# Gate projection of a mixer layer as two units of seven block products

## The reference

```python
u = rms_norm(h, g_mix)
z = u @ w_in                     # columns: q_a k_a v_a | q_b k_b v_b | f_b | gate_logits (2 x 1024)
y_a = sliding_window_attention(q_a, k_a, v_a, sinks) @ w_br_swa
y_b = forgetting_attention(q_b, k_b, v_b, f_b + b_forget) @ w_br_fox
gates = sigmoid(gate_logits)     # (tokens, 2, 1024)
mixed = gates[:, 0] * y_a + gates[:, 1] * y_b
h = h + mixed @ w_mix_out
```

## Time and profile before

| | us |
|---|---|
| median of 3 runs | 1800.6 (1798.06 to 1803.86) |
| profiled execution, its own time | 1800.78 |
| its span, first to last instruction | 1799.0 |
| TensorE busy | 1758.1 (98% of the span) |
| VectorE busy | 1027.4 (57%) |
| ScalarE busy | 671.0 (37%) |
| GpSimd busy | 266.1 (15%) |

### The profile page before, as it was taken

The page is one execution under the profiler, slowest core; times in us unless marked ns, Lnnn a source line. Parts: engine busy times, 40 slices in busy tenths (PEclk is TensorE's granted clock), DMA queues, the critical chain, the costliest instruction groups (busy, mean ns, idle before and its releaser), DMA issues.

```text
span 1799.0 us, 21080 instructions
## 1 busy us (share of the span) xinstructions
PE 1758.1 (98%) x8533; PEld 1479.4 (82%) x8533; DVE 1027.4 (57%) x1377; ACT 671.0 (37%) x1049; POOL 266.1 (15%) x350
## 2 busy tenths in 40 slices
PE   7999999999899999999999999999999999999998
PEld 7888888888899888887888888888887788888886
DVE  5432144432798444489957965984887256445423
ACT  4322244442798431453223323323344234222212
POOL 2000021210687125100000000000002132000101
PEclk9999999999999999999999999999999999999999
DMA  5434524214662454175173246227211112111232
GB/s 177 135 109 138 176 82 129 83 59 113 157 142 48 140 183 180 46 277 180 65 260 120 94 166 255 75 76 290 98 47 36 49 69 100 65 52 43 72 115 94
DMA packets 107600, 215.65 MB, mean 120 GB/s; under 512 B 7984, under 2 KB 28016, under 8 KB 105072
## 3 DMA queue, kind: packets, MB, share of 16 engines
q1 hardware_dynamic: 107504, 214.31, 35.7%
HBM read 170.21 MB, written 44.07 MB: 119 GB/s over the span
## 4 chain that ended last, share of the span: by engine, by line
PE 85%; DVE 5%; DMA 3%; ACT 2%; POOL 2%; issue 1%; SPq 1%; POOLq 0%; ACTq 0%; DVEq 0%
PE PS L649 16%; PE PS L651 16%; PE PS L650 16%; PE PS L883 10%; PE PS L884 10%; PE PS L885 10%; PE PS L625 3%; DVE WB L1705 1%; PE PS L753 1%; POOL TF L1990 1%; PE PS L798 1%; DMA kb_scratch<-STG 1%; SPq L2084 1%; DVE PFL L1379 1%; DMA KO<-kb_scratch 1%
## 5 line engine op out<-in xcount | busy, mean ns | idle before, releaser
L649 PE MATMUL PS<-UH,RHL 128*128 128x512 f32 (+1 forms) x768 | 294.3, 383 | 4.1 <-DVE UL L1379 2.2
L651 PE MATMUL PS<-UH,RHL 128*128 128x512 f32 (+1 forms) x768 | 290.3, 378 | 0.0
L650 PE MATMUL PS<-UL,RHL 128*128 128x512 f32 (+1 forms) x768 | 290.2, 378 | 0.0
L989 ACT ACTIVATE WH<-WB 128x2048 fp32r<-128x2048 f32 x56 | 107.3, 1916 | 295.1 <-PE PS L885 239.7
L1379 DVE TENSOR_TENSOR WB<-WB,WH 128x2048 fp32r<-128x2048 f32 x56 | 128.2, 2290 | 99.6 <-ACT WH L989 99.6
L883 PE MATMUL PS<-WH,AH 128*128 128x512 f32 x448 | 175.0, 391 | 4.0 <-DVE H L1666 2.3
L883 PE MATMUL PS<-AH,WH 128*128 128x512 f32 x448 | 174.6, 390 | 0.0
L885 PE MATMUL PS<-WH,AL 128*128 128x512 f32 x448 | 174.4, 389 | 0.0
L884 PE MATMUL PS<-WB,AH 128*128 128x512 f32 x448 | 174.3, 389 | 0.0
L885 PE MATMUL PS<-AH,WB 128*128 128x512 f32 x448 | 174.3, 389 | 0.0
L884 PE MATMUL PS<-AL,WH 128*128 128x512 f32 x448 | 174.3, 389 | 0.0
(11 more groups left out here) (219 smaller groups left out, 3249.5 us busy)
## 6 DMA issues: line engine op xcount, KB each, us to landing
WB<-in_w_ff SPq DMA_DIRECT2D x32, 1024.0 KB, 9.2
AH<-uf_scratch SPq DMA_DIRECT2D x21, 1024.0 KB, 5.3
AL<-uf_scratch SPq DMA_DIRECT2D x21, 1024.0 KB, 7.5
RAW<-in_w_in SPq DMA_DIRECT2D x32, 512.0 KB, 3.6
H<-in_x SPq DMA_DIRECT2D x16, 512.0 KB, 9.2
gates_scratch<-GST SPq DMA_DIRECT2D x32, 256.0 KB, 2.2
G<-gates_scratch SPq DMA_DIRECT2D x32, 256.0 KB, 2.9
RAW<-in_pool_in_w SPq DMA_DIRECT2D x16, 512.0 KB, 3.2
```

What stands on the lines that cost most here:

```text
L649: pe.matmul(o_ap, sh, mh, start=first, stop=False)
L650: pe.matmul(o_ap, sh, ml, start=False, stop=False)
L651: ins = pe.matmul(o_ap, sl, mh, start=False, stop=last)
L989: return act.activation(dst, src, ACT.Copy, **more)
```

## The change

The 2 x 1024 gate columns become two units (`u` = 0, 1), each the product of a 2 x 2 block matrix of weights (`A11` to `A22`, 512 x 512) with one of tokens (`B11` to `B22`, quarters of `UH` and `UL`). Seven products (`p` = 1 to 7) take the place of eight; their operands are four blocks and four sums of each side: `S1` to `S4` of weights, `T1` to `T4` of tokens.

What it adds, by place:

- Ahead of the stage: DVE rebuilds the four token blocks in float32 (`TU`, in the space of `H`), makes `T1` to `T4` of them (two of the four between tiles 2, 3, 4 and 5 of the `VA` loop), ACT and DVE split these into `TH` and `TUL`, and SP stores the four blocks and the four sums, both parts, into scratch (16 DMAs of 1 MB). Weight blocks are read whole (1 MB each, four for a unit). `S` sums of unit 0 are made on DVE during the `kb` stage. The second half of the tokens of `kb` comes first. `queries(0)` waits until all `T` are stored.
- In the stage: 14 steps (`g_order`) of four results each, 12 matmuls a result, 48 a step, 672 in all. Three products go on in the banks of the one before (`g_goes_on`). From step 2 on the token side of a step is read back from scratch, in two DMAs of 1 MB (`load_side`), issued in the step before: the first part at its start, the second after the store of its first result. The results of all 14 steps are stored (56 of 256 KB, four places `GST`). ACT and DVE split one weight operand of 128 x 2048 a step (`gate_high`, `gate_low`). The windows are spread over 112 steps; the distance of two windows is 5.65 steps, not 6.75.
- After it: the tokens are read back whole (`load_again`), the halves of `S_vb` change places, and the four places of the ring in which its weights lie are others.
- In the branch stage: a gate is the sum or difference of two stored products. SP reads four DMAs a half in place of two (`GX`), DVE makes the sum (`gates_of`, 128 x 1024) ahead of the sigmoid, those of `j + 1` between `y_second` and the low part of `j`.

The core of the diff:

```diff
-        S_gt = [slab512(w_in, 0, 2312 + 512 * j) for j in range(4)]
+        g_order = [(0, p) for p in (2, 1, 6, 7, 5, 3, 4)] + [(1, p) for p in (1, 6, 7, 2, 5, 3, 4)]
+        g_goes_on = (6, 7, 3)
+        gate_of = {(0, 0): (1, 2, ALU.add), (0, 1): (6, 3, ALU.add), (1, 0): (7, 4, ALU.subtract), (1, 1): (7, 5, ALU.add)}
```

TensorE, the stage:

```diff
-            for s in range(4):
-                for j in range(4):
-                    bs = [2 * (j % 2), 2 * (j % 2) + 1]
-                    for h in range(2):
-                        take(bs[h], *gate_copied.of(s, j, h))
-                    products([by_columns(S_gt[s], j, h, bs[h], gate_sum, (s, j, h), u_is("mix", 7)) for h in range(2)], range(8),
-                             [S_gt[s]] if j == 3 else (),
-                             {k: (lambda n=8 * (4 * s + j) + k: windows(n)) for k in range(8)})
+            for n in g_steps:
+                fresh = g_order[n][1] not in g_goes_on
+                (mh, ml), wl = g_side(n), g_form(n)[1]
+                for s in range(4):
+                    q = slice(P * s, P * s + P)
+                    take(s, *gate_copied.of(n, s))
+                    on.wait_ge(*gw_low.of(n))
+                    if n >= 2:
+                        on.wait_ge(*ug_in[n % 2].of(n, 1))
+                    for k in range(4):
+                        wh = g_high(n)[:, k, q]
+                        pe.matmul(bank(s), wh, mh[:, k, :], start=(k == 0 and fresh), stop=False, skip_group_check=True)
+                        pe.matmul(bank(s), wh, ml[:, k, :], start=False, stop=False, skip_group_check=True)
+                        ins = pe.matmul(bank(s), wl[:, k, q], mh[:, k, :], start=False, stop=(k == 3), skip_group_check=True)
+                        if k == 1:
+                            windows(8 * n + 2 * s)
+                    ins.then_inc(*gate_sum.up(n, s))
+                    windows(8 * n + 2 * s + 1)
```

ScalarE, ahead of the stage and in it:

```diff
+            turned_high("T4")
+            gate_high(0)
+            projected("kb", 1)
...
+            for n in g_steps:
+                if n < 13:
+                    gate_high(n + 1)
+                for s in range(4):
+                    for step in (8 * n + 2 * s, 8 * n + 2 * s + 1):
+                        for v in swa_steps[step]:
+                            window(*v)
+                    on.wait_ge(*gate_sum.of(n, s))
+                    on.wait_ge(*(gate_out[s].of(n - 1, s) if n else t_out.all()))
+                    copy(GST[s][:, :], bank(s)).then_inc(*gate_copied.up(n, s))
```

VectorE, the token sums and the VA loop:

```diff
             split_to(S_qa.idx[-1] + 4)
+            for n, q in u_blocks.items():
+                high, low = u_quarter(*q)
+                dve.tensor_tensor(TU[:, t_place[n], :, :], high.bitcast(F32), low.bitcast(F32), ALU.add).then_inc(*t_sum.up(n))
             for j in range(4):
                 spill(("qa", j, 1), j)
...
+            t_sums("T1", "B12", "B11")
+            t_sums("T3", "B22", "B12")
...
             for t in ts:
+                if t in (3, 5):
+                    t_sums(*(("T2", "B22", "T1") if t == 3 else ("T4", "T2", "B21")))
                 b, vs = (6 + t) % 8 if t < 6 else t, VS[t % 2]
```

VectorE, the stage:

```diff
+            for n in g_steps:
+                for k in range(8):
+                    if k == 1 and n < 13:
+                        if n == 6:
+                            gate_wide_sum(1, "S4")
+                        gate_low(n + 1)
+                    if n == 4 and k in (3, 5):
+                        gate_wide_sum(1, "S1" if k == 3 else "S3")
+                    if n == 5 and k == 3:
+                        gate_wide_sum(1, "S2")
```

SyncE, ahead of the stage:

```diff
+            on.wait_ge(*spill_sum.of("kb", 3, 1))
+            on.wait_ge(*ug_out.all())
+            gate_block(0, "A21")
+            gate_block(0, "A22")
             for v in spills[16:20]:
                 spill(v)
+            store_turned("T4")
+            on.wait_ge(*t_out.all())
             queries(0)
             for v in spills[20:24]:
                 spill(v)
...
             for s in spill_out:
                 on.wait_ge(*s.all())
             sp.dma_start(BIAS[:, :, :], A["c_bias"]).then_inc(*bias_in.up())
```

SyncE, the stage:

```diff
+            for n in g_steps:
+                u, p = g_order[n]
+                for s in range(4):
+                    if s < 2 and 1 <= n < 13:
+                        load_side(n + 1, s)
+                    if s == 2 and n in (1, 2, 3):
+                        gate_block(1, {1: "A21", 2: "A11", 3: "A12"}[n])
+                    if s == 3 and n == 1:
+                        gate_block(1, "A22")
...
+                    for step in (8 * n + 2 * s, 8 * n + 2 * s + 1):
+                        if ("queries", NT - 1, 0) in swa_steps[step]:
                             on.wait_ge(*w_biased.of(NT - 1, 1, 1))
                             queries(1)
+                    on.wait_ge(*gate_copied.of(n, s))
+                    sp.dma_start(gates_d[u, p - 1, s, :, :], GST[s][:, :]).then_inc(*gate_out[s].up(n, s))
```

The branch stage, VectorE and then SyncE:

```diff
+            def gates_of(j, hf):
+                on.wait_ge(*g_in[hf].of(j, 1, 1))
+                if j:
+                    on.wait_ge(*y_second.of(j - 1, hf))
+                dve.tensor_tensor(G[hf][:, :, :], GX[hf][0][:, :, :], GX[hf][1][:, :, :], gate_of[j // 4, hf][2]).then_inc(
+                    *g_summed.up(j, hf))
+
+            gates_of(0, 0)
+            gates_of(0, 1)
             for j in ts:
...
                     dve.tensor_tensor(y[:, 1, :], bank(b + 2), G[hf][:, 1, :], ALU.mult).then_inc(*y_second.up(j, hf))
+                    if j < 7:
+                        gates_of(j + 1, hf)
                     on.wait_ge(*mix_high.of(j, hf))
...
                 if j < 7:
                     for hf in range(2):
-                        on.wait_ge(*y_second.of(j, hf))
+                        on.wait_ge(*g_summed.of(j, hf))
                         fetch_gates(2 * j + 2 + hf)
```

More of the change, by code:

```diff
@@ L133, in scratch @@
             return nc.dram_tensor(f"{name}_scratch", shape, F32, kind="Internal").ap()
-        gates_d, h2_d = scratch("gates", [16, P, D]), scratch("h2", [P, NT, D])
+        gates_d, h2_d = scratch("gates", [2, 7, 4, P, 512]), scratch("h2", [P, NT, D])
+        ug_d = {n: scratch(f"ug{n}", [2, P, 2048]) for n in ("B11", "B12", "B21", "B22", "T1", "T2", "T3", "T4")}
         qa_d, qb_d, kb_d = (scratch(n, [4, 2, P, D]) for n in ("qa", "qb", "kb"))
@@ new lines, in block @@
+        def block(name, off, dt=F32):
+            return at(name, off, [P, 4, 512], dt)[:, :, :]
+        g_order = [(0, p) for p in (2, 1, 6, 7, 5, 3, 4)] + [(1, p) for p in (1, 6, 7, 2, 5, 3, 4)]
+        g_steps = range(len(g_order))
+        g_step = {v: n for n, v in enumerate(g_order)}
+        g_goes_on = (6, 7, 3)
+        g_wide = {1: "A11", 2: "A12", 3: "S4", 4: "A22", 5: "S1", 6: "S2", 7: "S3"}
+        g_tokens = {1: "B11", 2: "B21", 3: "B22", 4: "T4", 5: "T1", 6: "T2", 7: "T3"}
+        g_place = [{"A11": "R5", "A12": "R2", "A21": "a", "A22": "b", "S1": "c", "S3": "a", "S2": "d", "S4": "R2"},
+                   {"A11": "R5", "A12": "d", "A21": "R0", "A22": "R3", "S1": "a", "S3": "R0", "S2": "c", "S4": "R2"}]
@@ new lines, in build, with g_form @@
+        g_spot = []
+        for m, dt in enumerate((F32, F32R)):
+            spot = {f"R{n}": block(f"GR{n}{m}", 8 * K * n, dt) for n in range(6)}
+            for n, (off, j) in {"a": (0, 0), "b": (32 * K, 0), "c": (0, 1), "d": (32 * K, 1)}.items():
+                spot[n] = quarter(f"G{n}{m}", OU + off, j, 1, dt)
+            g_spot.append(spot)
+        def g_form(n):
+            place = g_place[g_order[n][0]][g_wide[g_order[n][1]]]
+            return g_spot[0][place], g_spot[1][place if n else "R0"]
@@ new lines, in g_high, with u_quarter, g_side @@
+        def g_high(n):
+            return g_spot[1]["R3" if n == 0 else "R1" if n % 2 else "R4"]
+        def u_quarter(j, h):
+            return tuple(v[:, 4 * j:4 * j + 4, 512 * h:512 * h + 512] for v in (UH, UL))
+        def g_side(n):
+            return u_quarter(0 if n % 2 else 1, 0)
+        u_blocks = {"B11": (0, 0), "B12": (0, 1), "B22": (1, 1), "B21": (1, 0)}
+        TU = at("TU", OH, [P, 4, 4, 512])
+        TUL = at("TUL", OH, [P, 4, 4, 512], F32R)
+        TH = block("TH", OX + 32 * K, F32R)
@@ new lines, in build @@
+        t_place = {"B11": 0, "B12": 1, "B21": 2, "B22": 3, "T1": 0, "T3": 1, "T4": 2, "T2": 3}
+        t_order = ["T2", "T3", "T1", "T4"]
+        t_sum = signal("t_sum", [(n,) for n in ("B11", "B12", "B22", "B21", "T1", "T3", "T2", "T4")])
+        t_high, t_low = signal("t_high", [(n,) for n in t_order]), signal("t_low", [(n,) for n in t_order])
+        t_out = landing("t_out", [(n, m) for n in t_order for m in range(2)])
+        ug_out = landing("ug_out", [(n, m) for n in u_blocks for m in range(2)])
@@ new lines, in build @@
+        ug_in = [landing(f"ug_in{i}", [(n, m) for n in g_steps[2 + i::2] for m in range(2)]) for i in range(2)]
+        u_again = [landing(f"u_again{h}", [(n, m) for n in ("B12", "B22") if h for m in range(2)] or
```

(9 more changed lines are left out.)

289 lines of the change are left out of this document (186 added, 103 removed).

## The result

The changed kernel took 1818.5 us (median of 4 runs, 1817.2 to 1820.1) against 1799.8 for the kernel before (4 runs): ratio 1.0102, 95% interval 1.009 to 1.0115. So it is 1.0% slower. I had forecast 1799.5 with a range of 1789 to 1809; the result lies outside. The profiled execution took 1820.1, with a span of 1818.3.

The account below looks back on a forecast made before the run. TensorE, busy 1758.1 of 1799.0 us, was taken as the bound. Terms -21.8 + 4.4 + 6.8 + 1.5 + 1.4 + 2.2 + 1.0 + 3.5 = -1.0 gave 1799.5 us, range 1789 to 1809.

Parts of the forecast that it names:

- 96 matmuls: Gate stage: 768 matmuls become 672, at 0.2267 us each, all on TensorE's path: 21.8 us less.
- C: Rival: gate matmuls start farther apart, or moved splits harm the forgetting attention: 1802 to 1804; chance 0.08 with unknown.
- VA loop: Two token sums on VectorE before tiles 3 and 5 delay the first qb product: cost 4.4 us, bounds 3.9 and 4.6.
- Step 2: Gate stage entry: TensorE waits for the second part of T2 read back: 6.8 us, bounds 4 and 11.
- Rival A: Gate stage entry: the reads keep up and no clock falls, 1789.2 us; chance 0.28 with its half-way cases.
- Step 3: Gate stage: the second part for this step lands at 233.3, wanted at 231.8: cost 1.5 us, bounds 0 and 4.
- B: Rival: in the gate stage the second part is late in every step, 1810.6 or 1821.6 us; chance 0.14.
- Second QS: Gate stage, step 7: TensorE waits 3.9 us for QS against 1.7 before: cost 2.2 us, bounds 1 and 4.
- Branch stage: Near 600: eight reads and VectorE's sums delay the first y products: cost 3.5 us, bounds 2 and 5.
- Clock: TensorE's clock falls behind the long wait of step 2: cost 1.4 us, bounds 0 and 1.7.
- Window events behind longer splits: Gate stage: windows wait behind 1.92 and 2.29 us splits, 2.5 us in all: cost 1.0, bounds 0 and 5.
- Forgetting attention: Stage given no cost in the sum; harm of 2 to 4 us from moved splits stood only under rival C.

Follow-up runs that it names:

- e18: The change with VA sums behind the loop, early step-2 read, later windows and forgetting-attention splits, long operations in halves, second value product 0.25 step later: 1793.6 us.
- e5b: The change with VectorE's low part of a weight operand made on a quarter of the columns, so the computation is changed: 1810.2 us.
- e6: The change with ScalarE's high part of a weight operand made on a quarter of the columns from step 3, so the computation is changed: 1815.2 us.
- e19: e18 without its halves, the second value product still 0.25 step later: 1804.6 us.
- e3: The change with the two weight splits at the start of the forgetting attention moved some 180 events later: 1817.0 us.
- e13: The change with each long operation of the gate stage placed behind a window event after which the next turn is two to four steps off: 1830.1 us.
- e2: The change with both parts of T2 for step 2 read back as soon as step 0 is done, ahead of BIAS: 1815.4 us.
- e15: e14 without the early read and with the windows at their old distance, one and a quarter step more between the eighth and ninth: 1814.6 us.
- e14: The change with the edits of e1, e2, e3 and e13 together, and windows begun two steps later at a distance of 5.55 steps: 1807.9 us.
- e1: The change with the token sums T2 and T4 moved behind the VA loop, nothing else: 1811.7 us.

## Why the prediction was wrong

The mechanism of the sum was right: matmuls saved, less new waits, less the clock behind them. The sizes of three terms were not.

- *96 matmuls, -21.8.* Right. The busy times of the change (with its clock) and of e18 show it, and in the gate product matmuls 26 apart start at 192.22 and 198.11, 0.2265 us each, so "the gain is not there" (C) is out.
- *VA loop, +4.4.* Measured 4.1 at 98.85.
- *Step 2, +6.8.* Measured 7.75. BIAS went out at 207.15, not 204.7, the second part at 215.46, not 212.5, and landed 7.3 later. The nearness owes something to chance: the two falls of the clock ahead of the stage, which I had not reckoned, put TensorE 3.0 us later (first gate product at 192.22, not 189.2) and SyncE's list about as much (QS issued at 189.55, not 186.5), and the wait is the difference of the two. Rival A is out. Step 3 had no wait (1.5 forecast), and UL or UH waits did not repeat, so B is out too.
- *Second QS.* 2.9 where I had 3.9. *Branch stage.* 2.1 where I had 3.5, though most gate sums took 2.34 us and not the 1.2 I used.
- *Clock, +1.4.* **The step that failed most.** I had priced one fall, behind the one long wait. Measured: 13.8, ten times that and nearly ten over my upper bound of 1.7. The clock fell at seven places, behind waits of 2 to 8 us and at one (147) with only 0.4 and 0.4 before it. I had read in the earlier trace rows what a fall costs and not asked how many of my own new waits might bring one. The rule that I weighed there ("TensorE: Matmul & The Clock Gate", "HAM oscillation", in the Trainium skill) says that bursts of matmuls with gaps of waiting keep falling to the low clock; I applied it to one wait. The trace agrees at six of the seven places, and not at the waits for QS (2.9), PFL (2.34) and SM (1.87), which brought no fall.
- *Window events behind longer splits, +1.0.* **The second.** Measured 8.8 (PRL 10.3 in place of 1.5), above my bound of 5. I had set the lengths of the splits against average room (VectorE 86 of 224 us) and a small part of the old wait. But a window is a chain through all four engines with 1.5 to 2 steps of slack, and one 2.29 us operation holds up two links of it, VectorE's own and, as the timeline at 330 shows, GpSimd's. e5b (6.1 us less) and e6 (4.4 less) show that these operations make most of the waits, and e18 against e19 that they need not. What is left in e5b, 2.7 above the kernel before, is open.
- *Forgetting attention, 0.* Measured 4.2 more (PFL 2.3, SM 1.9), the 2 to 4 that I had put under rival C as an alternative to the sum rather than in it. e3 shows that the splits make the part of PFL; what the wait for SM hangs on wasn't settled.

With 13.8, 8.8 and 4.2 in their places, and the other terms as measured, the sum is -21.8 + 4.1 + 7.8 + 13.8 + 1.2 + 8.8 + 2.1 + 4.2 = +20.2, against a span of +19.3. The range failed with them: its bad end added up bounds of which two were too low by 12 and 4 us.

## What to carry to other kernels

Where TensorE is busy all the time, price each new wait with the fall of the clock that it may bring, and count the waits: here 27 us of new waits came with 14 us of lost clock, though not each wait brought a fall. A longer operation on an engine with much idle time still has to fit between two links of the tightest chain through that engine; when it is moved, keep both its due times in view (e13). Cutting it up paid where the other waits were mended (11.0 us), and hardly on the change itself (1.2). Moving one transfer ahead of others in a full queue mends its own wait and makes theirs, so mend what they feed in the same edit: the early read alone gave 3.1 us (e2), with the windows later 6.7 (e15 to e14).

## What the runs showed of the chip that I had not expected

- The clock fell without a wait of note. Around 146 TensorE waited 0.41 and 0.36 us in the changed kernel, in the kernel before and in e1 alike, between some short matmuls; the granted clock fell only in the changed kernel. What went before differs, the wait of 4.1 us and the fall at 99: nine of the ten profiles with that wait show the second fall, and none of the nine without it (the kernel before among them). It isn't bound to follow: e6 has the wait and the first fall, and a clock of 1.00 from 102 to 160.
- A GpSimd operation of 0.22 us took 2.23 and 2.19 us while VectorE ran a 128x2048 operation of 2.29 with both inputs in SBUF, and 1.12 to 1.13 beside the halves of e18. The Trainium skill says why ("SBUF — State Buffer", "Who interferes with whom": a VectorE instruction with two SBUF inputs and a GpSimd one that reads SBUF can't run together, and the later waits out the earlier). The lengths agree: at 330 GpSimd's operation ends 0.08 us behind VectorE's. It seems to go the other way too: VectorE's sum of two gate reads took 1.22 us at the least and 2.34 at the median, in the stage where GpSimd adds `Y`. At 622.44 such an addition of 1.28 us starts, at 622.46 a sum that takes 2.34.

```profile
L1765 DVE TENSOR_TENSOR G<-GX,GX x16: 1224/2342/2349, 608.3 to 679.5; 128x1024 f32<-128x1024 f32 x16
```
